# A fused two-block transformer kernel: the second pair of modulation slabs is loaded and multiplied ahead of the first projection's first products

## The chip, the cores and the metric

The kernel runs on one core of a Trainium2 chip. That core has five engines: TensorE (PE in the profile, its weight loads PEld) multiplies matrices, VectorE (DVE), ScalarE (ACT) and GpSimd (POOL) work elementwise, and SyncE (SP) issues most transfers. They meet through semaphores alone. The metric is the device time of one execution in microseconds (us); less is better.

## The reference

The reference is one transformer block with a mixture of experts, and behind it two more layers that mix tokens, all of them in float32 on 256 tokens of 1024 features. Only its start matters here. The condition `c`, one vector of 1024, is passed through silu and multiplied with a matrix of 1024 x 6144; the result, `mod`, is cut into six vectors of 1024, of which the first two are `shift1` and `scale1`:

```python
mod = jax.nn.silu(c) @ w_ada[l] + b_ada[l]
shift1, scale1, gate1, shift2, scale2, gate2 = jnp.split(mod[:, None, :], 6, axis=-1)
h = rms_norm(x, g_norm1[l]) * (1.0 + scale1) + shift1
proj = h @ w_in[l]
```

Behind that come the two attentions of the block, their output projections, the router, 64 experts of which each token takes 8, and the two further layers.

## The kernel before

**Weights.** All weights are kept in memory as slabs of 1 MB (128 partitions x 2048 numbers), in the order in which the kernel wants them. In the fast memory there is a ring of 11 slots of a slab each. Code of TensorE's program asks for a slab where it uses it (`take_slab`, line 585, and `new_slab`, line 476), and so the order of asking is the order of loading. The n-th slab takes the slot of slab n - 11. SP's program (`load`, line 1637) walks through the slabs in that order: it waits until the slab that had the slot has been given back (`given_back`, line 1630) and then issues the load (line 1659). It does not skip: while it waits for one slot, the loads behind it are not issued.

**Three kinds of slabs at the start.** A modulation slab (`ada1`, 0 to 7) holds 256 columns of the modulation's matrix: slabs 0 to 3 make `shift1`, 4 to 7 make `scale1`. `ada_slab` (line 590) multiplies one with the silu of `c`, 8 products on quarters of the array, and the slab's slot is given back when its products are done. A projection slab (`in`, 0 to 7 here) holds 256 columns of `w_in`, and is multiplied with the tiles of `h`, which the program calls `hT` and `h1`: 8 feature tiles k of 128 x 256 tokens. A projection slab is given back only when its last product, that of k = 7 for the second half of the tokens, is done. A side slab (`ada1`, 8 to 23; `leave_to_vector`, line 616) is not for TensorE: DVE weighs it with a row of `c` (`weigh_slab`, line 2276; two long instructions to a slab), and gives it back.

**From modulation to h.** Slabs j and j + 4 are a pair, and make the batch `("first", j)`: shift and scale of two of the eight feature tiles. When the pair has been multiplied, ACT copies the result out of its bank (`ada_quarters`, line 1798, the copy is line 1804), TensorE folds the four quarters together (`ada_fold`, line 642, products on line 647), DVE adds the bias, makes the gain and scales two tiles of `x` (`ada`, line 2202, and `scale`, line 2236), and ACT adds the shift (`shift`, line 1817, on line 1821). Then `h1` has two tiles more. ACT's program has these steps in the order copy, two shifts, copy, two shifts, and DVE's likewise.

**The order of TensorE's work at the start** is written out by hand (lines 853 to 876). `two_ks(s, i)` multiplies projection slab s with feature tiles 2i and 2i + 1 for both halves of the tokens: four products, which the profile counts as 8, as it does all products of float32. It waits for those tiles and, at its first use, for the slab. Each slab s has two banks that collect its sums (0 and 1 for slab 0, 2 and 3 for slab 1), which ACT empties when they are complete (lines 1848 and 1849), so that slabs 3 and 4 can use them again.

**What ACT issues.** With the fourth batch ACT issues transfers of its own on its queue (lines 1831 to 1841): constants, vectors, a row of `c` in a copy for each partition (`c_row`), the biases of the attention, and two more rows. The silu of `c_row` (line 1852) stands in ACT's program between the emptying of projection slab 0's banks and that of slab 1's, and DVE's weighing waits for it (line 2288).

The first loads are, before the change: modulation 0, modulation 4, projection 0, modulation 1, 5, projection 1, modulation 2, 6, 3, 7, projection 2, projection 3, side slabs 0 and 1, projection 4, side slabs 2 and 3, projection 5, and so on.

Of the kernel before, what the change touches and what calls it, by code (L numbers as in the profile page):

```python
# [148 lines left out]
def build(nc, x_d, ctx_d, consts_d, consts2_d, vecs_d, pos_d, rpb_d, spat_d, router_d, crow_d, crow2_d, slabs_d, exp_d, out_d):  # L149
    with ExitStack() as ctx:  # L150
# [5 lines left out]
        def S(name):  # L156
            if name not in sems:
                sems[name] = ctx.enter_context(nc.semaphore(name))
            return sems[name]
# [29 lines left out]
        def cc(name, a=0, b=None):  # L189
            src, at = (cs, C_AT) if name in C_AT else (cs2, C2_AT)  # L190
            lo, hi = at[name]
            if src is cs2 and lo >= DFT_W:
                src, lo, hi = cs_late, lo - DFT_W, hi - DFT_W
            return src[:, lo + a:(hi if b is None else lo + b)]
# [160 lines left out]
        def done(eng, name):  # L355
            b, n = place[name]
            eng.wait_ge(psum_done[b], n + 1)

        def bk(name):
            return bank[place[name][0]]  # L360
# [128 lines left out]
        def ends(n, end):  # L489

            slab_end[n] = end
            let_go.append(n)
            if given:
                given[0].append(n)
# [37 lines left out]
        def ada_batch(which, j):  # L532

            if which == "ada1" and j < 8:
                return ("first", j % 4), j // 4
            for n, (w, lo, count) in ADA_BATCHES.items():
                if w == which and lo <= j < lo + count:
                    return n, j - lo

        def batch_size(batch):  # L540
            return 2 if batch in FIRST_BATCHES else ADA_BATCHES[batch][2]
# [7 lines left out]
        OTHER = (12, 13, 20, 14, 15, 16, 17, 18, 19, 21, 22, 23)  # L549
        PASSES = [(i, t, side) for i, j in enumerate(OTHER) for t in range(2) for side in range(2 if j < 20 else 1)]  # L550
        PASSES_TO = [sum(n <= i for n, _, _ in PASSES) for i in range(len(OTHER))]
        other_slabs = []
        READ_EARLY, DUMPED_EARLY = 10, 20
# [8 lines left out]
        def _(pe):  # L562
            mmul = nc.tensor.matmul

            def open_group(name, b):

                if uses[b]:
                    pe.wait_ge(psum_done[b], uses[b])
                place[name] = (b, uses[b])
                uses[b] += 1  # L570
                return bank[b]

            def close_group(ins, name):
                ins.then_inc(psum_full[place[name][0]], 1)
# [10 lines left out]
            def take_slab(src):  # L585

                n = ask(src)
                return arrived(n), n

            def ada_slab(which, j):  # L590

                w, n = take_slab((which, j))
                w = w.rearrange("p (k c) -> p k c", k=8)
                batch, r = ada_batch(which, j)
                first, last = r == 0, r == batch_size(batch) - 1
                if first:
                    open_group((batch, "quarters"), 6)
                o = bk((batch, "quarters"))
                at = 15 - r if which == "ada1" else 22 - 2 * r  # L600
                for kk in range(2):
                    for g in range(4):
                        mm = mmul(o[32 * g:32 * g + 32, 0:256], (silc if which == "ada1" else silc2)[:, 4 * kk + g, at:at + 32],
                                  w[:, 4 * kk + g, :], start=first and kk == 0, stop=last and kk == 1)
                    if kk == 1:
                        if last:
                            close_group(mm, (batch, "quarters"))
                            ends(n, (batch, "quarters"))
                        else:
                            ada_reads[0] += 1  # L610
                            mm.then_inc(S("ada_read"), 1)
                            ends(n, ("ada_read", ada_reads[0]))
# [29 lines left out]
            def ada_fold(batch, b=7):  # L642

                done(pe, (batch, "quarters"))
                o = open_group((batch, "columns"), b)
                for t in range(2):
                    mm = mmul(o[:, 32 * t:32 * t + 32], quarters[:, t * P:(t + 1) * P], cc("fold"), start=True, stop=True)
                close_group(mm, (batch, "columns"))
# [180 lines left out]
            def first_inputs(slab, t, ks):  # L829

                name = (f"qk{slab}", t)
                if slab not in in_at:
                    in_at[slab] = take_slab(("in", slab))[1]
                o = open_group(name, 2 * slab + t) if ks[0] == 0 else bk(name)
                for k in ks:
                    h_tile("h1", k)
                    mm = mmul(o[:, 0:256], hT[:, k, t * P:(t + 1) * P], eight(in_at[slab])[:, k, :], start=(k == 0), stop=(k == KT - 1))  # L837
                if ks[-1] == KT - 1:
                    close_group(mm, name)
                    if t == 1:  # L840
                        ends(in_at[slab], name)
# [7 lines left out]
            def two_ks(slab, i):  # L849
                for t in range(2):  # L850
                    first_inputs(slab, t, (2 * i, 2 * i + 1))
# [2 lines left out]
            ada_slab("ada1", 4)  # L854
            pe.wait_ge(S("fold_in"), 16)
            ada_fold(("first", 0))
            two_ks(0, 0)
            ada_slab("ada1", 1)
            ada_slab("ada1", 5)
            ada_fold(("first", 1))  # L860
            two_ks(1, 0)
            two_ks(0, 1)
# [2314 lines left out]
```

## Time and profile before

| | us |
|---|---|
| runs: median (lowest to highest of 3) | 1056.69 (1054.32 to 1059.71) |
| profiled execution, its own time | 1058.16 |
| its span, first to last instruction | 1056.3 |
| TensorE busy in the span | 1012.3 |
| DVE / ACT / POOL busy | 454.9 / 282.6 / 160.5 |
| moved in transfers | 336.59 MB, mean 319 GB/s |

The profile is one execution as the hardware profiler saw it. Times in its rows count from the start of the span. A granted clock of 1.00 is TensorE's full clock, 2.4 GHz, and 0.50 its other level, 1.2 GHz. The share of transfers is the mean busy share of the core's 16 transfer engines; packets can overlap a little, so that a full stretch shows 1.01 or more. Queue q1 carries what SP issues, q10 what ACT issues. The idle time in brackets is that of the engine just before the instruction, with what ended it.

### The profile page before, as it was taken

The numbers are of one execution on the slowest core, as the hardware profiler recorded it, in microseconds if no ns is written. First come the engines' busy times: TensorE is split into PE (matmuls) and PEld (weight loads), VectorE is DVE, ScalarE is ACT, GpSimd is POOL, SyncE is SP. The second block draws the span as 40 slices with busy tenths as digits, with TensorE's granted clock in tenths as the row PEclk, the third lists the DMA queues.
The fourth block names the chain that finished last, engine by engine and source line by source line (L and its number), as shares of the span: only waits on it lengthen the run. The fifth ranks groups of instructions, "written<-read, shape, count | busy, mean of one in ns | idle before, by whom it ended". The sixth has DMA issues, their size and how long they took to land.

```text
span 1056.3 us, 16485 instructions
## 1 busy us (share of the span) xinstructions
PE 1012.3 (96%) x6434; PEld 712.6 (67%) x6434; DVE 454.9 (43%) x1112; ACT 282.6 (27%) x656; POOL 160.5 (15%) x154
## 2 busy tenths in 40 slices
PE   6998999999989999999899999999979999999998
PEld 4776867788546556465356556655459998998577
DVE  1366998686621321212112121221425652657941
ACT  3224465302511111212111211113222111213951
POOL 0000030225000000000000000001015963391001
PEclk9999999999999999999999999999989999999999
DMA  9999998469999999999999999999996434320001
GB/s 382 328 421 421 421 420 323 166 248 358 369 398 411 415 422 420 420 421 421 421 421 421 406 421 421 420 421 421 419 418 264 160 121 159 119 82 1 1 2 41
DMA packets 50463, 336.59 MB, mean 319 GB/s; under 512 B 5776, under 2 KB 8464, under 8 KB 10832
## 3 DMA queue, kind: packets, MB, share of 16 engines
q1 hardware_dynamic: 46976, 329.01, 76.8%
q10 hardware_dynamic: 3024, 4.79, 1.6%
q0 software_dynamic: 384, 1.70, 0.5%
q8 instruction: 53, 0.87, 0.3%
q14 instruction: 26, 0.21, 0.1%
HBM read 334.43 MB, written 1.05 MB: 318 GB/s over the span
## 4 chain that ended last, share of the span: by engine, by line
PE 85%; DMA 7%; DVE 4%; issue 2%; ACT 1%; SPq 0%; DVEq 0%; ACTq 0%
PE bank L1286 15%; PE bank L1447 11%; PE bank L1329 7%; PE bank L1241 5%; DMA ring<-experts 5%; PE bank L1107 4%; PE bank L1131 3%; PE bank L1174 3%; PE bank L1545 3%; PE bank L990 3%; PE bank L696 3%; PE bank L1598 2%; DMA ring<-stream 2%; PE bank L837 2%; PE bank L763 2%; PE bank L1007 2%
## 5 line engine op out<-in xcount | busy, mean ns | idle before, releaser
L1286 PE MATMUL bank<-ring,arena 128*32 128x512 f32 (+1 forms) x1112 | 175.8, 601 | 9.9 <-DMA ring<-experts 9.9
L1286 PEld LDWEIGHTS bank<-ring,arena 128*32 128x32 f32 (+1 forms) x1112 | 51.1, 120 | 114.7 <-issue 114.5
L1734 POOL TENSOR_TENSOR hT<-hT 128x256 f32<-128x256 f32 x30 | 28.5, 950 | 610.5 <-ACT hT L1815 608.8
L1329 PE MATMUL bank<-ring,conds 128*32 128x512 f32 (+1 forms) x560 | 87.8, 596 | 5.7 <-DMA ring<-experts 3.1
L2745 DVE TENSOR_TENSOR yhalf<-bank,yhalf 128x512 fp32r<-128x512 f32 x48 | 33.2, 692 | 80.0 <-ACT yhalf L2049 80.0
L2730 DVE SCALAR_TENSOR_TENSOR conds<-bank,gcol,conds 128x256 f32<-128x256 f32 x24 | 11.6, 484 | 123.8 <-ACT conds L2041 109.6
L2008 ACT ACTIVATE arena<-bank,mod 128x256 f32<-128x256 f32 x96 | 40.3, 471 | 78.2 <-PE bank L1107 77.9
L1329 PEld LDWEIGHTS bank<-ring,conds 128*32 128x32 f32 (+1 forms) x560 | 25.8, 119 | 49.9 <-issue 43.5
L1107 PE MATMUL bank<-picked,halves 128*128 128x256 f32 x384 | 57.8, 294 | 0.4 <-ACT arena L2008 0.4
L1107 PEld LDWEIGHTS bank<-picked,halves 128*128 128x128 f32 x384 | 49.0, 189 | 10.2 <-issue 9.1
L2488 DVE SCALAR_TENSOR_TENSOR resid<-bank,mod,resid 128x256 f32<-128x256 f32 x40 | 18.8, 482 | 80.3 <-PE bank L1174 25.4
L2041 ACT ACTIVATE conds<-bank 128x256 f32<-128x256 f32 x24 | 9.2, 383 | 144.5 <-PE bank L1286 144.5
L696 PE MATMUL bank<-hT,ring 128*128 128x256 f32 x192 | 42.5, 381 | 4.1 <-ACT arena L1901 2.2
L1131 PE MATMUL bank<-yhalf,selT 128*128 128x512 f32 x184 | 46.3, 394 | 0.0
L2283 DVE CUSTOM_DVE_ANT_1 hT<-ring,hT,ve 128x1024 bf16<-128x1024 f32 x32 | 40.3, 1307 | 10.5 <-DMA ring<-stream 10.5
L2049 ACT CAST yhalf<-bank 128x512 fp32r<-128x512 f32 x48 | 28.1, 585 | 60.5 <-PE bank L1329 60.5
L1241 PE MATMUL bank<-hT,ring 128*128 128x256 f32 x192 | 43.2, 382 | 0.0
L2737 DVE COPY conds<-bank 128x256 f32<-128x256 f32 x24 | 10.2, 425 | 76.3 <-PE bank L1316 76.3
L696 PEld LDWEIGHTS bank<-hT,ring 128*128 128x128 f32 x192 | 36.1, 190 | 10.1 <-DMA ring<-stream 5.4
L1815 ACT ACTIVATE hT<-resid 128x256 f32<-128x256 f32 x48 | 18.0, 411 | 88.6 <-DVE resid L2488 88.4
L1447 PE MATMUL bank<-hT,ring 128*128 128x128 f32 x304 | 40.5, 277 | 0.7 <-ACT hT L1821 0.7
L1241 PEld LDWEIGHTS bank<-hT,ring 128*128 128x128 f32 x192 | 36.0, 190 | 7.2 <-issue 2.5
(487 smaller groups left out, 1833.2 us busy)
## 6 DMA issues: line engine op xcount, KB each, us to landing
ring<-experts SPq DMA_DIRECT2D x187, 1024.0 KB, 13.1
ring<-stream SPq DMA_DIRECT2D x118, 1024.0 KB, 13.3
ring<-experts SPq DMA_DIRECT2D x8, 512.0 KB, 8.9
resid<-x SPq DMA_DIRECT2D x1, 1024.0 KB, 5.2
arena<-c_rows ACTq DMA_DIRECT2D x2, 512.0 KB, 12.2
resid<-ctx ACTq DMA_DIRECT2D x1, 1024.0 KB, 9.2
keys_room<-experts SPq DMA_DIRECT2D x1, 1024.0 KB, 13.0
arena<-stream SPq DMA_DIRECT2D x1, 1024.0 KB, 14.4
```

The source lines that it names most:

```text
L696: mm = mmul(o[:, 0:n_tok], w[:, k, t * P:(t + 1) * P], hT[:, k, 0:n_tok], start=(k == 0), stop=(k == KT - 1))
L990: mm = mmul(o[:, 0:256], w[:, 512 * k + P * t:512 * k + P * t + P], yT[:, y0 + k, :], start=(k == 0), stop=(k == 3))
L1107: mm = mmul(o[:, 256 * (d % 2):256 * (d % 2) + n], halves[:, q, t, P * d:P * d + P], picked[:, t, 0:n], start=(t == 0 and q == 0), stop=(t ...
L1131: mmul(bank[b][:, :], selT[:, b // 2, :], yhalf[:, q, 512 * (b % 2):512 * (b % 2) + 512], start=m == 0 and q == 0, stop=False)
L1174: mm = mmul(o[:, 0:T], eight(n)[:, k, P * (d % 2):P * (d % 2) + P], y_c[:, k, :], start=(j == 0), stop=(j == KT - 1))
L1241: mm = mmul(o[:, 0:T], w[:, k, P * (i % 2):P * (i % 2) + P], hT[:, k, T:2 * T], start=(k == 0), stop=(k == KT - 1))
L1286: mm = mmul(o[at:at + n_slots, :], xg_of(m, kk)[:, at:at + n_slots], w[g][:, k, :], start=(kk == 0), stop=(kk == KT - 1))
L1329: mm = mmul(o[at:at + n_slots, :], aT[:, f, at:at + n_slots], w[g][:, 2 * c + f, :], start=(f == 0), stop=(f == 1))
L1447: mm = mmul(o[:, at:at + P], lhs[:, k, :], rhs[:, k, :], start=k == 0, stop=k == 3)
L2008: last = a.activation(to[:, i, 0:n], bk(("xg", j, c))[:, 256 * i:256 * i + n], ACT.Identity, bias=mod1[:, 24 + 2 * c + i:25 + 2 * c + i])
L2283: v.tensor_tensor_reduce(out=products[:, 2 * t:2 * t + 2, :].rearrange("p a (b c) -> p a b c", b=2), in0=ring[:, slot_of[n], 1024 * t:1024 ...
L2745: last = v.tensor_tensor(yhalf[:, 1, 512 * c:512 * c + 512], bk(("y", m, c))[:, :], yhalf[:, 0, 512 * c:512 * c + 512].bitcast(F32), ALU.s ...
```

## The change

The first use of projection slab 0, its products with feature tiles 0 and 1, is moved behind modulation slabs 1 and 5 in TensorE's program. With it the order of loading changes: these two modulation slabs become the third and the fourth load, and projection slab 0 the fifth. All else is the same.

```diff
             ada_slab("ada1", 4)
             pe.wait_ge(S("fold_in"), 16)
             ada_fold(("first", 0))
-            two_ks(0, 0)
             ada_slab("ada1", 1)
             ada_slab("ada1", 5)
+            two_ks(0, 0)
             ada_fold(("first", 1))
             two_ks(1, 0)
             two_ks(0, 1)
```

## Rows read from the trace of the kernel before

**Rows 1.** The page: transfer shares in 40 slices of 26.4 us; the chain by engine
```profile
DMA  9999998469999999999999999999996434320001
...
PE 85%; DMA 7%; DVE 4%; issue 2%; ACT 1%; SPq 0%; DVEq 0%; ACTq 0%
```

**Rows 2.** TensorE in order of time: start, us, line, tiles, count [idle before, releaser]
```profile
13.23 1.93 PE L603 MATMUL bank<-ring,conds 128*32 128x256 f32 x32
...
18.03 2.57 PE L837 MATMUL bank<-ring,hT 128*128 128x256 f32 x8 [1.67 <-ACT hT L1821]
...
20.53 2.96 PE L603 MATMUL bank<-ring,conds 128*32 128x256 f32 x32
...
23.99 0.63 PE L647 MATMUL bank<-cs,quarters 128*128 128x32 f32 x4 [0.50 <-ACT quarters L1804]
...
24.46 5.43 PE L837 MATMUL bank<-ring,hT 128*128 128x256 f32 x24
```

**Rows 3.** Windows: stretch, us, busy us by engine, granted clock, transfer share, GB/s
```profile
15.20:18.00 2.80, 0.60 (x4) 0.53 (x5) 2.26 (x5) 1.00 (x3) 0.00 (x0) 1.00 1.01 421
...
18.00:20.50 2.50, 2.47 (x8) 1.66 (x8) 0.00 (x0) 0.28 (x1) 0.00 (x0) 0.75 1.01 419
...
20.50:23.50 3.00, 2.99 (x33) 1.24 (x32) 0.00 (x0) 0.00 (x0) 0.00 (x0) 0.64 1.03 429
```

**Rows 4.** The chain of waits, 50 to 125 us: start, us, what
```profile
57.41 22.83 DMA ring<-stream
...
80.29 3.72 PE bank L904 x16
...
106.21 14.05 PE bank L696 x64
```

**Rows 5.** Windows, as rows 3, of two longer stretches
```profile
37.00:45.00 8.00, 8.00 (x46) 6.84 (x39) 3.19 (x15) 2.67 (x8) 0.00 (x0) 1.00 0.76 221
...
57.00:177.00 120.00, 113.85 (x675) 89.10 (x674) 98.96 (x226) 54.70 (x138) 13.38 (x18) 1.00 1.01 421
```

**Rows 6.** TensorE in order of time, as rows 2, 60 to 90 us
```profile
64.61 7.17 PE L711 MATMUL bank<-ring,hT 128*128 128x256 f32 x32 [0.28 <-DMA ring<-stream]
...
72.83 7.17 PE L696 MATMUL bank<-hT,ring 128*128 128x256 f32 x32 [1.04 <-DMA ring<-stream]
```

**Rows 7.** SP and transfers at 3.6 us: issue; KB, us from issue to landing
```profile
3.42 0.47 SPq L1659 DMA_DIRECT2D ring<-stream  x1
...
ring<-stream SPq DMA_DIRECT2D x1, 1024.0 KB, 14.9
```

**Rows 8.** SP's waits, 13 to 46 us (total, times, longest); its issues, 40 to 60
```profile
SPq L1659 <- PE bank L837: 28.5, 1, 28.5
...
44.09 14.23 SPq L1659 DMA_DIRECT2D ring<-stream  x12
```

**Rows 9.** ACT's queue (q10), 45 to 49, then 50 to 52 us: packets, MB, share
```profile
q10 hardware_dynamic: 767, 0.88, 107.3%
...
q10 hardware_dynamic: 75, 0.29, 36.8%
```

**Rows 10.** ACT's issues; transfers issued 30 to 44 us: KB each, us to landing
```profile
37.45 0.33 ACTq L1831 DMA_DIRECT2D cs<-consts  x1
...
38.78 0.66 ACTq L1834 DMA_DIRECT2D hT<-c_row  x1
...
cs<-consts ACTq DMA_DIRECT2D x1, 585.0 KB, 3.5
...
hT<-c_row ACTq DMA_DIRECT2D x1, 512.0 KB, 6.1
```

**Rows 11.** ACT and DVE in order of time, as rows 2, 45 to 62 us
```profile
46.10 1.06 ACT L1852 ACTIVATE hT<-hT 128x1024 f32<-128x1024 f32 x1
...
54.33 1.28 DVE L2283 CUSTOM_DVE_ANT_1 hT<-ring,hT,ve 128x1024 bf16<-128x1024 f32 x1 [3.99 <-DMA ring<-stream]
...
59.62 1.28 DVE L2283 CUSTOM_DVE_ANT_1 hT<-ring,hT,ve 128x1024 bf16<-128x1024 f32 x1 [2.13 <-DMA ring<-stream]
```

## The prediction

> **What bounds the kernel now.** I read the page first: the chain that ended last is TensorE for 85% of the span, and the row of transfer shares is full except in slices 7 to 9, 158 to 238 us, and at the end [rows 1]. TensorE busy says little, because the change touches only the first 60 us; what counts is which wait ends last there. So the second view is TensorE's instructions in order of time [rows 2]. The reader is to see three things: after the first fold (it ends at 18.03 - 1.67 = 16.36) TensorE idles 1.67 us for the first two feature tiles of h1; then come the first products and the second pair of modulation slabs, and another 0.50 us goes to the copy ahead of the second fold; and the two pieces between those gaps are slow, 2.57 us for 8 products and 2.96 for the slab pair, where 24 products take 5.43 later (1.81 per 8) and the earlier slab pair took 1.93. The third view, the windows, says why: the granted clock is 0.75 and 0.64 of full there [rows 3], so it sat at the lower of its two levels, 1.2 GHz, for part of it, after a stretch in which TensorE was busy 0.60 of 2.80 us.
>
> The fourth view is the chain of waits from 50 to 110 us [rows 4]: TensorE until 57.0, and then one load, issued at 57.41, that lands at 80.24 and on which the last projection tiles start at 80.29. Transfers run at 421 GB/s with a share of 1.01 from 57 to 177 us [rows 5], and TensorE waits for slabs in that stretch (0.28 us at 64.61, 1.04 at 72.83 [rows 6]). So between 57 and 80 us the landing of slabs sets the time. TensorE's gain before 57 is worth only as much as the slabs come earlier. Behind 80 the path runs over the latent sums, the reciprocal on DVE, the latent squares on ACT and back to TensorE at 106.21, and from there TensorE is the chain, with transfers that have room soon after (slices 7 to 9). A shift at 80 is therefore carried to the end.
>
> **The change part by part.** No instruction, byte or transfer is added or removed: 8 products move behind two slabs' 32 instructions in TensorE's order, and, since slabs are asked for in that order, one load moves behind two others in SP's queue.
>
> *TensorE's order.* Now: fold, wait 1.67, products 2.57, slab pair 2.96, wait 0.50, fold. After: the pair starts at 16.4 and ends near 18.3 at full clock (1.93); the products need h1 (ready at 18.0) and their own slab; the second copy runs on ACT beside the products, and the second fold follows without its wait. Saved: 1.67 + 0.50 = 2.17 us. If the clock no longer falls, since the emptiest stretch is filled, 2.57 - 1.81 = 0.76 and 2.96 - 1.93 = 1.03 go as well: 3.96 us. ACT is no obstacle: its second copy stands behind the two shifts, of which the first let TensorE go at 18.03, and the pair ends only then.
>
> *The landings it needs.* The first projection slab becomes the fifth load instead of the third. The fifth load is issued at 3.42 and lands 14.9 us later, at 18.3 [rows 7], when the products are due; the two modulation slabs take places three and four and land earlier. I price this at nothing; with a landing 0.5 us later it costs 0.5. TensorE thus reaches the slab of the sixth projection tiles 2.2 to 4.0 us earlier; I take 3.5.
>
> *The ring.* This is what decides. The ring has 11 slots, and SP waits in order. The 12th and 13th loads take the slots of the first two modulation slabs, which are free once the first pair is through. The 14th takes the slot of the first projection slab, which is in use until its last products, and SP stands there 28.5 us, until 44.1 [rows 8]. Meanwhile the queue runs dry: from 37 to 45 us the transfers have a share of 0.76 and move 221 GB/s [rows 5], mostly small ones that ACT issues from 37.45 on [rows 10]. After the change slots three and four hold modulation slabs that are free near 17.3 and 18.3. So the 14th and 15th load are queued before 19 us, and only the 16th waits for the first projection slab, until about 44.1 - 3.5 = 40.6. Two slabs of 1.05 MB at 421 GB/s are 2 x 2.49 = 5.0 us of work, so the queue is full until 42. The empty part of the stretch, 8 x (1 - 0.76) = 1.9 us, or 2.0 against the 1.01 of a full one, is filled, and all that comes behind lands 2.0 us earlier. The rest is no gain: ACT's transfers have to be moved too, and while they were, from 45 to 49, ACT's queue alone had a share of 107% [rows 9].
>
> Bounds: the gain is at most 5.0 us, if ACT's small transfers cost the stream nothing, and it can't exceed TensorE's own 3.96 plus the 1.3 us that it waits now for slabs between 57 and 80; at least 0, if the empty share moves elsewhere. The value is the accounting of the row itself, 2.0.
>
> *What is late next.* TensorE reaches the sixth projection slab near 60.3 but this lands near 64.6 - 2.0 = 62.6, so some 2 us of its gain turn into a wait there. The clock may fall as it did at 16 to 23 us; that cost 1.8 us, of which the wait of 1.04 ahead of the seventh slab, now TensorE's only slack, takes up more than half, so at most 0.8 us is lost at the landing near 78.
>
> *ACT's transfers.* ACT issues the constants (at 37.45 now) and the row of c (38.78) some 3.5 us earlier, but now behind two more slabs. The row of c lands today 6.1 us after its issue, at 44.9 [rows 10]; its silu gates ACT's next evictions and DVE's weighing of side slabs. The trace shows how the two queues share: the loads that SP issued from 44.09 on moved nothing before 49, while ACT's earlier transfers were served [rows 8, 9]; that is service nearly in the order of issue. Then constants and row (1.12 MB) come behind the 15th load: at the stream's 0.42 MB/us they land at 42.3 + 2.7 = 45.0 at the earliest, and with all of today's 44.9 - 37.45 = 7.4 us at 49.7 at the latest; I take the middle, 47.4. From that landing DVE needs 2.3 us until the silu is done (46.10 + 1.06 today) and about 6.2 for two side slabs, at two instructions of 1.28 each, and four short reductions, before it can begin the third side slab, which will be there at 59.62 - 2.0 = 57.6 [rows 11]. The waits that DVE has today (3.99 us for the second side slab, 2.13 for the third) are that cover. A landing up to 57.6 - 8.5 = 49.1 leaves the full gain, one at 51.1 none. I cost it at nothing; at the late end it is 0.6.
>
> The Trainium skill (DMA: Bandwidth & Descriptors, "Queues, rings and completion order") says that each DMA engine serves its queues in turn, packet by packet. By that rule the row of c would not stand behind the two slabs and the last rival below falls away. The stretch from 45 to 49 us, 107% for one queue with eight loads waiting in the other, speaks against it here, the 37% that ACT's queue had beside the stream from 50 to 52 us for it [rows 9]; the forecast's 2.0 us are the same by both, as the engines have no empty time either way.
>
> **The sum.** The profiled execution took 1058.16 us (span 1056.3 and 1.9 around it); less 2.0 it is 1056.2. It lies 1.5 above the median of the three runs, so for the median 1056.69 - 2.0 = 1054.7.
>
> **The rivals.**
> - *The stream gains more than its empty time* (22%): up to 4.0 us, TensorE's own gain: 1052.7. For: shares above 1 mean that packets overlap, and 37 to 45 moved only 221 GB/s, so ACT's slow packets may fit in beside large ones. Against: beside the stream (50 to 52) ACT's 0.29 MB took 37% of the time, 0.39 MB/us, no less than the stream's own.
> - *Nothing reaches the end* (15%): 1056.7. TensorE's gain turns wholly into waits for slabs between 57 and 80 us. For: share 1.01 from 57 on. Against: the empty stretch ahead of it.
> - *The row of c comes too late* (8%): slower. Place: ACT's silu of it, ahead of the second projection slab's evictions and DVE's first side slab. Behind both slabs, and then beside the 16th load at the 0.29 MB in 2 us that ACT's queue got from 50 to 52 [rows 9], its 1.12 MB take 7.7 us in place of 2.7: 49.7 + 5.0 = 54.7, 3.6 past the 51.1 that leaves nothing, so 1056.69 + 3.6 = 1060.3. For: the 16th load is issued only 5 us after them. Against: what ACT issued first was served first. Each further microsecond costs one.
>
> **How the numbers follow.** The forecast has 55%, with its own range 1052.5 to 1057. What a measurement of this kernel can tell from no change is about 0.5%, 5.3 us; the three runs alone spread over 5.4. None of the cases reaches that by its mean. Faster by more than 5.3 us needs the first rival at its upper end and scatter: 12%. Slower by as much needs the last with a landing past 56, or scatter: 5%. Within: 83%. The range takes in the first rival's mean and 2 us of scatter below, and above the second with 2: 1050.5 to 1058.8, with the last and some scatter left out.
>
> **What would show it.** TensorE without the gaps of 1.67 and 0.50, granted clock near 1.0 from 16 to 23.5; SP's long wait for the first projection slab shorter than 28.5 and ended near 41; a transfer share near 1 from 37 to 45; the load that now lands at 80.24 landing near 78.2; a new wait of about 2 us ahead of the sixth projection slab; TensorE's restart at 106.21 near 104.2. Wrong would be: that landing unmoved (nothing gained), moved by 4 (the first rival), or DVE idle for ACT's silu past 50 us and the third side slab weighed after 59.6 (the last).

## The result, and the profile after

The changed kernel took 1071.74 us (median of 4 runs, 1066.90 to 1072.49) against 1058.20 for the kernel before beside it (4 runs, 1054.32 to 1061.78): ratio 1.0112, 95% interval 1.0073 to 1.0151. It is slower by more than 0.5%, where 1054.7 was forecast. The profiled execution took 1071.74 (span 1069.9), 13.6 more than the one of before; at 46 us it is still ahead, at 70 us 13.2 behind.

TensorE in order of time, changed kernel (start, us, line, operation, tiles, shapes, count, idle before and what ended it), the answer to [rows 2, 6]:

```profile
15.65 1.93 PE L603 MATMUL bank<-ring,conds 128*32 128x256 f32 x32
18.45 1.99 PE L837 MATMUL bank<-ring,hT 128*128 128x256 f32 x8 [0.87 <-DMA ring<-stream]
20.93 5.45 PE L837 MATMUL bank<-ring,hT 128*128 128x256 f32 x24
36.00 10.61 PE L837 MATMUL bank<-ring,hT 128*128 128x256 f32 x48
60.83 9.63 PE L885 MATMUL bank<-ring,hT 128*128 128x256 f32 x32 [14.22 <-ACT pr L1849]
70.30 7.07 PE L683 MATMUL bank<-ring,hT 128*128 128x256 f32 x32
77.20 7.07 PE L711 MATMUL bank<-ring,hT 128*128 128x256 f32 x32
```

The kernel before, from its last fold on:

```profile
39.50 10.61 PE L837 MATMUL bank<-ring,hT 128*128 128x256 f32 x48
49.94 7.07 PE L885 MATMUL bank<-ring,hT 128*128 128x256 f32 x32
57.15 7.17 PE L683 MATMUL bank<-ring,hT 128*128 128x256 f32 x32
```

The first four lines of the changed kernel are what was forecast, but for a wait of 0.87 us: the slab pair at full clock behind the fold, no gaps of 1.67 and 0.50, and the products behind the last fold begin at 36.0, 3.5 us earlier than they did. Then comes a hole of 14.22 us. L837 is projection slabs 0 to 2, L885 is slab 3, L683 slab 4, L711 slab 5. Slab 3 collects in the banks of slab 0, so it may start only when ACT has emptied these (L1848, L1849), and ACT has not. The windows show the two ends of it: the stretch in which transfers had a share of 0.76 [rows 5] is full now, and TensorE's clock sat at the lower level (0.50 of full is 1.2 GHz) from the hole until 65 us, so slab 3 took 9.63 us where the next took 7.07 (columns as in [rows 3]):

```profile
37.00:45.00 8.00, 8.00 (x39) 7.04 (x38) 0.47 (x2) 0.91 (x2) 0.00 (x0) 1.00 1.02 410
47.00:61.00 14.00, 0.17 (x1) 0.20 (x2) 2.40 (x13) 0.96 (x4) 0.00 (x0) 0.56 1.03 389
61.00:65.00 4.00, 4.00 (x10) 3.19 (x11) 1.36 (x3) 3.42 (x7) 0.00 (x0) 0.50 1.04 365
```

Why ACT was late is in its own row of instructions (ACTq marks the issuing of a transfer):

```profile
33.95 0.33 ACTq L1831 DMA_DIRECT2D cs<-consts  x1
...
35.28 0.64 ACTq L1834 DMA_DIRECT2D hT<-c_row  x1
...
38.19 5.82 ACTq L1839 DMA_DIRECT2D bias_room<-rpb  x1
44.04 15.95 ACTq L1841 DMA_DIRECT2D arena<-c_rows  x2
60.04 0.38 ACT L1848 ACTIVATE arena<-bank 128x256 f32<-128x256 f32 x1 [22.01 <-issue]
62.55 1.06 ACT L1852 ACTIVATE hT<-hT 128x1024 f32<-128x1024 f32 x1
```

ACT stood 22 us in issuing: the second bias transfer took 5.82 us to issue, the two later rows 15.95, where each of the same issues took 0.33 to 0.66 in the kernel before. The copies that TensorE waited for stand behind these in ACT's order. The chain of waits says the same (start, us, what):

```profile
38.19 5.82 ACTq L1839
...
44.72 15.27 ACTq L1841
...
60.83 9.63 PE bank L885 x32
```

And what ACT had issued before was late too. Transfers by issue (KB each, median us from issue to landing), against 3.5 and 6.1 in [rows 10]:

```profile
bias_room<-rpb ACTq DMA_DIRECT2D x2, 438.0 KB, 31.7
...
cs<-consts ACTq DMA_DIRECT2D x1, 585.0 KB, 9.5
hT<-c_row ACTq DMA_DIRECT2D x1, 512.0 KB, 24.7
```

The row of c, issued at 35.28, landed at 59.98, 15 us later than before. The two queues from 36 to 60 us (q1 is SP's, the stream; q10 is ACT's: packets, MB, share of the 16 engines):

```profile
q1 hardware_dynamic: 1131, 8.23, 85.4%
q10 hardware_dynamic: 1133, 1.36, 16.7%
```

Over the span: projection slab 3 is 10.9 us late (49.94 to 60.83) and slow, slab 4 13.2 late (57.15 to 70.30); the waits for slabs of [rows 6] are gone, so the restart of [rows 4] comes at 116.84, 10.6 late. The clock falls once more there (64 products take 15.74 us for 14.05), which makes it 12.3; a longer wait for the experts' loads at 322 us makes it 14.6, and at the end it is 13.6.

### The profile page after: what moved, and what is told of

The parts are those of the page before. It is cut to its first block, busy times and chain, and to the rows that moved or that the text cites. A ratio compares the mean times of both kernels' runs of the same rounds, so it can differ in the third digit from the quotient of the medians.

```text
span 1069.9 us, 16485 instructions
## 1 busy us (share of the span) xinstructions
PE 1014.3 (95%) x6434; PEld 714.2 (67%) x6434; DVE 455.9 (43%) x1112; ACT 282.8 (26%) x656; POOL 163.7 (15%) x154
## 4 chain that ended last, share of the span: by engine, by line
PE 83%; DMA 7%; DVE 4%; ACTq 2%; issue 2%; ACT 1%; SPq 1%; DVEq 0%
PE bank L1286 14%; PE bank L1447 11%; PE bank L1329 7%; PE bank L1241 5%; DMA ring<-experts 5%; PE bank L1107 4%; PE bank L696 3%; PE bank L1131 3%; PE bank L1174 3%; PE bank L1545 3%; PE bank L990 3%; PE bank L1598 2%; PE bank L763 2%; PE bank L1007 2%; PE bank L637 2%; PE bank L749 2%
## 5 line engine op out<-in xcount | busy, mean ns | idle before, releaser
L1734 POOL TENSOR_TENSOR hT<-hT 128x256 f32<-128x256 f32 x30 | 28.5, 950 | 612.9 <-ACT hT L1815 611.2
L1329 PEld LDWEIGHTS bank<-ring,conds 128*32 128x32 f32 (+1 forms) x560 | 26.0, 121 | 53.1 <-issue 47.2
## 6 DMA issues: line engine op xcount, KB each, us to landing
ring<-experts SPq DMA_DIRECT2D x187, 1024.0 KB, 13.4
```

The lines of the kernel that those rows point to most:

```text
L1329: mm = mmul(o[at:at + n_slots, :], aT[:, f, at:at + n_slots], w[g][:, 2 * c + f, :], start=(f == 0), stop=(f == 1))
```

## The experiments

Two theories to begin with. **A:** the transfer engines take a piece from each queue in turn; as long as SP's queue isn't dry, ACT's small pieces get one turn per 8 KB of stream, and the row of c, the issues behind it and the evictions behind those are late. **B:** the share goes by bytes or by order of issue, and the cause is elsewhere: in the products' new order, in the new order of loads as such, or in ACT's issuing. In the first four expectations A is called theory Q, there with ACT's held issues as what costs the time; rival P is the order of the products, and rival C is that the late landing of the row of c costs the time by itself. (Some expectations call L885 the second projection slab; it is slab 3.)

**Loads in the changed order, products in the old.** The two modulation slabs are asked for ahead of the first products, and used where they were:

```diff
+            asked = ask(("ada1", 1)), ask(("ada1", 5))
             two_ks(0, 0)
-            ada_slab("ada1", 1)
-            ada_slab("ada1", 5)
+            ada_slab("ada1", 1, asked[0])
+            ada_slab("ada1", 5, asked[1])
```

> The two modulation slabs are asked for ahead of the first projection slab, as in the changed kernel, but TensorE multiplies in the order of the kernel before. Theory Q (queue): with the stream's queue never dry, the bias transfers that ACT issues, small pieces, get only one piece for each 8 KB piece of the stream; ACT's next issue instructions then do not finish, ACT sits in them some 15 to 21 us, the first projection's banks are emptied late, and TensorE waits for them. So: 8 to 15 us slower than before, an issue on ACT of over 10 us, TensorE waiting some 10 us ahead of the fourth projection slab. Rival P (products): the order of TensorE's work is the cause; then this kernel is within 2 us of before and ACT's issues are short.

**Products in the changed order, loads in the old.**

```diff
             ada_fold(("first", 0))
+            early_in[0] = ask(("in", 0))
             ada_slab("ada1", 1)
             ada_slab("ada1", 5)
             two_ks(0, 0)
```

> TensorE multiplies in the order of the changed kernel, but the first projection slab is still asked for, and so loaded, third. Theory Q: SP waits for its slot as before, the stretch from 37 to 45 us stays free for ACT's transfers, ACT's issues take under 1 us each; the time is 0 to 2 us below before, since the slabs' landings between 57 and 80 us move little. Rival P: 10 to 14 us slower, as the changed kernel.

Measured, beside 1058.54 of before: loads alone 1065.42 (10 runs; eight of them 1065.2 to 1066.9, two at 1053.3 and 1055.8), ratio 1.0045 (1.0011 to 1.0079); products alone 1058.66, ratio 0.9994 (0.9969 to 1.0020). The loss comes with the order of loads, in eight of ten executions and not all of it. With the products alone TensorE's gain turns into waits for slabs, as the forecast's second rival had it (TensorE in order of time):

```profile
55.11 7.17 PE L683 MATMUL bank<-ring,hT 128*128 128x256 f32 x32 [1.11 <-DMA ring<-stream]
64.09 7.17 PE L711 MATMUL bank<-ring,hT 128*128 128x256 f32 x32 [1.81 <-DMA ring<-stream]
```

With the loads alone the row of c lands at 50.1, 5 us late, its silu runs 4 us late, and the two later rows, issued last, hold ACT a second time (ACT in order of time, in an execution of the longer kind):

```profile
50.13 1.06 ACT L1853 ACTIVATE hT<-hT 128x1024 f32<-128x1024 f32 x1 [1.72 <-DMA hT<-c_row]
...
73.89 1.06 ACT L1855 ACTIVATE arena<-arena 128x1024 f32<-128x1024 f32 x1 [12.30 <-DMA arena<-c_rows]
```

The issue of over 10 us and the wait ahead of slab 3 that were expected did not come: ACT's longest issues took 1.48 us, and 2.33 for two, and TensorE's wait, 8.74 us, lies inside slab 5, for copies that stand behind the silu of the later rows.

**ACT's held issues taken out of the way.** The changed kernel, with the bias and the two later rows issued behind the emptying of slab 1's banks and their silu moved back. If ACT's issuing is the root, the loss goes.

```diff
+                if s == 1:
+                    ...  # the four act.dma_start of bias and rows
...
-            act.wait_ge(S("bias_in"), 64)
-            ...  # silu of the two rows, now behind the vna copies
```

> The changed kernel, with ACT's four issues of bias and rows moved behind the eviction of the second projection slab, and the wait for them behind the evictions of the value tiles. Theory Q: nothing stands between the first fold's work and the evictions any more; TensorE has no wait of 14 us ahead of the fourth projection slab; 0 to 4 us below before, by the 2 us of transfer time that the full queue gains. Rival C (row of c): its landing, 60.0 us in the changed kernel, is what counts, through the silu ahead of the second projection slab's evictions; if it still lands past 55, TensorE waits at the fifth projection slab instead and the kernel stays 5 to 12 us slower.

1074.97 us, ratio 1.0149 (1.0116 to 1.0182): no better, as rival C had it. ACT in order of time:

```profile
59.53 1.06 ACT L1847 ACTIVATE hT<-hT 128x1024 f32<-128x1024 f32 x1 [16.75 <-DMA hT<-c_row]
...
61.50 0.64 ACTq L1851 DMA_DIRECT2D bias_room<-rpb  x1
62.17 0.66 ACTq L1851 DMA_DIRECT2D bias_room<-rpb  x1
62.86 2.86 ACTq L1853 DMA_DIRECT2D arena<-c_rows  x2
```

The row of c is as late as ever with nothing behind it in its queue, so the held issues don't make the row late; issued with the row gone, the same four take 4.2 us in place of 22. TensorE now gets through slab 3 and stops at slab 4, which needs slab 1's banks, emptied behind the row's silu: it starts 4.8 behind the kernel before, and loses 10.79 us more where the silu of the later rows, issued at 63, is awaited (TensorE in order of time):

```profile
61.92 9.26 PE L683 MATMUL bank<-ring,hT 128*128 128x256 f32 x32 [8.18 <-ACT pr L1844]
...
100.42 2.93 PE L656 MATMUL bank<-arena,ones 128*128 128x256 f32 x6 [10.79 <-ACT arena L1867]
```

**Bias and later rows from SP's queue**, issued ahead of its 16th load; ACT keeps constants, positions, vectors and the row of c.

```diff
+                if n == 15:
+                    ...  # the four transfers, by sp.dma_start
                 load(n)
```

> The changed kernel, with the same four transfers issued by SP in the stream's own queue, ahead of the 16th load. Theory Q: they are served in their turn without a share by pieces, ACT is never held, and the stream loses only their own time: 0 to 4 us below before, bias and rows landed by 58 us. Rival C: as in the run with ACT's later issues, 5 us or more slower if the row of c still lands past 55. If it is not the issuing queue but the sheer amount of transfers in this stretch: some 10 us slower as the changed kernel.

1060.33 us, ratio 1.0016 (0.9985 to 1.0046): most of the loss is gone. SP's queue carries small pieces itself while the row of c is on its way, and from 44 to 48 us equal turns are equal bytes:

```profile
q1 hardware_dynamic: 516, 0.50, 56.2%
q10 hardware_dynamic: 525, 0.47, 55.3%
```

The row lands at 53.1, still late.

The next two runs change the size of one side's pieces, and with it the number of its transfers, and nothing else. **The row of c in pieces of 512 B** (the changed kernel otherwise):

```diff
-                    act.dma_start(c_row, crow_d...).then_inc(S("vec_in"), 16)
+                    for h in (0, 128):
+                        act.dma_start(c_row[:, :, h:h + 128], crow_d...[:, :, h:h + 128]).then_inc(S("vec_in"), 16)
```

> The changed kernel with the row of c written in two transfers of 512 B pieces (1024 of them) in place of one of 1 KB pieces (512); the bytes, their place in ACT's queue and all of the order stay. Theory A (while the stream's queue holds loads, the engines take one piece of ACT's queue for each 8 KB piece of the stream, so a transfer's time goes by its count of pieces): 512 further pieces at the 49 per us of 52 to 60 us in the changed kernel, faster once the stream's queue is dry at about 64 us: 4 us at 49, the other 316 at about 150 per us, so the row lands at 66 to 67 us in place of 59.98, TensorE restarts 5 to 7 us later than at 60.83, and the kernel takes 1076 to 1080 us against 1071.74 of the changed one. Theory B (service by bytes, or by the order of issue, or the wait is in ACT's issuing): the row lands at about 60 us as before and the time stays at 1071 to 1073.

**The stream in pieces of 4 KB**, loads 11 to 22 (the changed kernel otherwise):

```diff
-                    sp.dma_start(room, w).then_inc(slab_in[slot], 16)
+                    for c in ((0, 1024), (1024, 2048)) if n in SPLIT else ((0, 2048),):
+                        sp.dma_start(room[:, c[0]:c[1]], w[:, c[0]:c[1]]).then_inc(slab_in[slot], 16)
```

> The changed kernel with loads 11 to 22 of the stream issued as two halves each, in pieces of 4 KB in place of 8 KB; bytes, order and ACT's transfers stay as they are. Theory A (one piece of ACT's queue for each piece of the stream): a pair of pieces takes 0.18 us of an engine in place of 0.32, so ACT's queue gets some 87 pieces per us in place of 49, the row of c lands at 48 to 52 us in place of 59.98, TensorE's second projection slab starts 8 to 10 us earlier than at 60.83, and the kernel takes 1062 to 1068 us against 1071.74; the 1280 pieces behind the row then last to about 65 us and may hold ACT again. Theory B (the share goes by bytes, or ACT's queue is served last whatever the pieces): the row stays at about 60 us, the time at 1071 to 1073.

With 512 B pieces the row landed at 68.2 (forecast 66 to 67); the kernel took 1073.19 us, below the 1076 to 1080 expected of it: slab 3 waits for ACT's issues, which were over at 62.7, and so starts 2.7 us later, where 5 to 7 were expected; what is late by the row comes only behind that. Queues from 52 to 60 us in that run:

```profile
q1 hardware_dynamic: 424, 3.08, 93.2%
q10 hardware_dynamic: 420, 0.21, 9.4%
```

With the stream in 4 KB pieces the row landed at 52.0 (forecast 48 to 52), slab 3 started at 51.04, and the kernel took 1066.58 us (5 runs; ratio 1.0072, 1.0045 to 1.0099), 5.2 less than the changed kernel, for no byte less. TensorE, and the queues from 52 to 60 us:

```profile
51.04 8.52 PE L886 MATMUL bank<-ring,hT 128*128 128x256 f32 x32 [4.33 <-ACT pr L1851]
```

```profile
q1 hardware_dynamic: 591, 2.14, 83.0%
q10 hardware_dynamic: 590, 0.50, 21.3%
```

Halving one side's piece moved the row by 8 us one way, halving the other's by 8 us the other way; the counts stay equal. The pieces alternate one by one, too: if those of the run with 512 B pieces, 52 to 60 us, are strung into 16 engines by their start and end times in the trace, 787 of 828 are followed by a piece of the other queue. By bytes or by order of issue neither would have moved it. Theory A is shown, but for what holds ACT's issues, which stays open (last section).

**What the order is worth with the row early.** All of ACT's transfers of 33.95 to 60 us go into SP's queue: constants, positions, vectors and the row ahead of load 13, bias and later rows ahead of load 15 (changed order), or all ahead of load 13 (order of before).

```diff
+                if n == 13:
+                    ...  # cs, rq, ve, c_row by sp.dma_start
+                if n == 15:
+                    ...  # bias and later rows by sp.dma_start
                 load(n)
```

> The changed kernel with all that ACT issues from 33.95 us on put into SP's queue: constants, positions, vectors and the row of c ahead of load 13, the bias and the two later rows ahead of load 15. Theory A (only the alternation of two queues of unequal pieces made the row late): the row lands with the stream, by about 45 to 50 us, no wait of 14 us is left before the second projection slab, and the 2.0 us of the prediction come through: 1054.5 to 1056.5 beside a kernel before of 1058.5 (ratio 0.996 to 0.998). Theory B (the changed order itself, with its clock or its landings, costs something that e4 still hid): at or above the kernel before, 1058 to 1062.

> The order of the kernel before, with all that ACT issued from 33.95 us on put into SP's queue ahead of load 13. Theory A: the dry stretch of the stream's queue beside ACT's (44 to 49 us) goes, and the row comes no later than its 44.9 us: 1 to 2 us faster, 1056.5 to 1057.5 beside 1058.5. If this alone gives as much as the changed order with the same edit, the changed order is worth nothing of itself. Theory B (moving these bytes ahead of loads 13 on only makes the slabs later): 1059 to 1061.

Beside 1059.19: changed order 1061.99, ratio 1.0016 (0.9993 to 1.0040), a miss for theory A's numbers; order of before 1057.79, ratio 0.9988 (0.9966 to 1.0009), 1.4 us less where 1 to 2 were expected, but not told from no change. The changed order's twelve executions are of two kinds, seven at 1061.9 to 1063.7 us and five at 1054.0 to 1057.5; the profiled one is of the longer kind. In it the row's silu ran at 42.9, and the evictions were not late. But 1.9 MB of bias and rows (2 x 438 and 2 x 512 KB) now stood ahead of projection slab 5 in the one queue:

```profile
64.01 10.10 PE L711 MATMUL bank<-ring,hT 128*128 128x256 f32 x32 [3.57 <-DMA ring<-stream]
```

It waited 3.57 us, and the clock fell behind the wait (0.66 of full from 60 to 70 us): 10.10 for 7.07. Here an early TensorE in front of landings that didn't come earlier bought a wait, and the wait cost the clock. So the last two runs take those bytes out of the stretch: **bias and later rows only ahead of load 33**, ACT's silu of them behind the square root of the latent heads, in the changed order and in the old one.

```diff
-                if n == 15:
+                if n == 33:
                     ...  # bias and later rows by sp.dma_start
```

> The changed order with constants, positions, vectors and the row of c in SP's queue ahead of load 13, the bias and the two later rows only ahead of load 33, and ACT's silu of those rows moved behind the square root of the latent heads (about 1.5 MB leave the stretch in which TensorE waits for slabs). Theory A (landings between 57 and 80 us set the pace, some 0.4 MB per us): 1.5 MB less ahead of them is up to 3.7 us; 1053 to 1055 beside 1058.5 (ratio 0.995 to 0.997). Theory B (TensorE's own work and its clock bind there once the row is early): no more than the changed order with all on SP, 1055 to 1056.5.

> The order of the kernel before with the edits of the run just ahead of it (constants, positions, vectors and the row of c in SP's queue ahead of load 13, the bias and the two later rows ahead of load 33, ACT's silu of those behind the square root of the latent heads): the two differ in the changed order alone. In the changed order that kernel took 1055.73 us, its TensorE began the products behind the first latent norm at 99.99 us. Theory A (with the row early and the landings out of the way, TensorE's early 2 to 3.7 us come through to that point): it begins at 102 to 104 us here, and the kernel takes 1056.5 to 1058. Theory B (the landings from 57 us on set that point whatever the order): 100 us here too, and 1055 to 1056. Theory C (a later bound, the experts' first transfers at 295 to 312 us, which gave back 4.3 of 5.5 us in that run, takes what there is): the point at 102 to 104 us and yet the same end within 0.5 us.

Changed order: 1055.73 beside 1059.19, ratio 0.9971 (0.9949 to 0.9993), the only version whose interval lies below the kernel before, though by less than the 0.5% that tells it from no change. Its time lies in theory B's range, 0.7 above theory A's; but the wait for projection slab 5 is gone, and the ratio is 0.0045 below that of the run with these bytes in the stretch, so they did cost time there. Order of before: 1058.40 beside 1059.48, ratio 0.9989 (0.9968 to 1.0010), with the restart where theory A had it and the time 0.4 above its range. TensorE restarts behind the latent squares (106.21 in [rows 4]) at 99.99 and at 102.41; here the changed order, then the order of before:

```profile
60.35 7.07 PE L711 MATMUL bank<-ring,hT 128*128 128x256 f32 x32
...
99.99 7.14 PE L696 MATMUL bank<-hT,ring 128*128 128x256 f32 x32 [3.77 <-ACT arena L1899]
...
304.87 3.64 PE L1329 MATMUL bank<-ring,conds 128*32 128x512 f32 x32 [2.06 <-DMA ring<-experts]
...
311.35 3.65 PE L1286 MATMUL bank<-ring,arena 128*64 128x512 f32 x16 [2.84 <-DMA ring<-experts]
```

```profile
102.41 15.92 PE L696 MATMUL bank<-hT,ring 128*128 128x256 f32 x64 [3.77 <-ACT arena L1899]
```

So in these two executions the order is worth 2.4 us at that point, once nothing waits for ACT's queue and the slabs come in time. At the end the two runs' ratios differ by 0.0018, some 1.9 us, with intervals that overlap: its worth there isn't settled. In this one profiled execution (1058.57, the highest of the twelve) the lead of 5.5 us that it had over the kernel before at 254 us was 3.9 at 275 and 1.2 at 312: part went in a stretch of low clock, the rest in waits for the experts' first loads, the last two lines of the changed order above. Whether that holds in the faster executions was not seen.

## Why the prediction was wrong

**TensorE's order: right.** 2.2 to 4.0 us were forecast, 3.5 taken; the products behind the last fold began 3.5 earlier, at a granted clock of 1.00 from 16 to 23.5 us. The size goes by the execution: over the traces these products begin at 35.9 to 36.2 with loads and products in the changed order, and at 38.1 to 39.8 with TensorE in the order of before, always some 26.3 to 26.6 us behind the first slab pair, which began anywhere from 11.9 to 13.2.

**The landings it needs: right.** Priced at nothing, for a landing at 18.3; the products began at 18.45. Their wait of 0.87 us is TensorE being early in that execution: its first slab pair began at 12.60 in place of 13.23, and in the three traces where it began at 13.4 or 13.5 there is no such wait.

**The ring: right as far as it shows.** SP's long wait for the first projection slab is 22.6 us in place of the 28.5 of [rows 8], and the share from 37 to 45 us is 1.02 in place of 0.76. Whether all behind it landed 2.0 us earlier can't be told from the changed kernel, whose TensorE waits for no slab between 30 and 125 us. But the empty stretch that was to be won was what had kept ACT's transfers quick: beside a dry stream they had the engines to themselves.

**ACT's transfers, costed at nothing: the step that failed.** It put the landing of the row of c at 45.0 to 49.7 and took 47.4, from "service nearly in the order of issue"; it was 59.98. That reading came from 45 to 49 us [rows 9], a stretch that began with the stream's queue dry. The right row stood beside it: from 50 to 52 us both queues had work, and ACT's moved 75 pieces in the 2 us. The prediction used that row too, but by its MB (0.29), which were pieces of 4 KB, of the later rows. Counted in pieces it is 37.5 per us, and then the row's own 512 pieces alone take 13.7 us beside the stream, in place of the 2.7 us by their bytes, or at most today's 7.4, that the step gave to constants and row together.

**ACT's issuing: not in the prediction at all.** It moved two transfers of ACT's queue in thought and left out the four issues behind them. These held ACT 22 us in its own order, so that slab 0's banks, ahead of the row's silu in ACT's order, were late as well as slab 1's. The run that moved them tells the shares at TensorE: a late row alone puts slab 4 back by 4.8 us, with the held issues it is 13.2.

**The last rival** (8%, 1060.3) had a place that is shown, ACT's silu ahead of slab 1's banks, the direction, and the sign: DVE waited 12.07 us for that silu, past 50 us. Its price of 3.6 us was the same count by bytes. Its "against", that what ACT issued first was served first, was the misread row.

The sentence on the Trainium skill (DMA: Bandwidth & Descriptors, "Queues, rings and completion order": each engine serves its queues in turn, packet by packet) drew the wrong conclusion from the rule. The runs agree with turns (1131 to 1133 pieces, 424 to 420, 591 to 590), and turns are just what makes the rival come true: a queue of small pieces beside one of large pieces is served evenly in pieces and badly in bytes.

## What to carry to other kernels

When a change keeps a queue full that used to run dry, look at what the other queue moved in that gap, and price it in pieces, not bytes: beside a full stream it gets about as many pieces as the stream does. A transfer of 512 KB in 1 KB pieces then costs as many turns as 4 MB of stream in 8 KB pieces. Look also at what stands behind the issuing of transfers on an engine that computes: once its queue is held, so are the copies that another engine waits for.

## What the runs showed that was not expected

- Equal turns are not the whole of it. Where the stream's queue had run dry, ACT's pieces went on alone for some time after the stream's loads were issued again: in the run with the loads alone, loads were issued at 46.14 and behind, and from 46 to 49 us the stream moved nothing while ACT's queue moved 622 pieces; the kernel before shows it too [rows 8, 9], with 987 pieces from 44 to 49 us. As an estimate from these counts, 39 to 62 pieces for each of 16 engines had been taken on before. No run here varied that.
- One order of loads gave two results, 1053 to 1056 and 1065 to 1067 us, in one set of ten runs with nothing between, and the run with all on SP's queue did likewise. Only the longer kind was profiled. That it hangs on whether ACT's pieces meet a dry queue is a guess.
- An issue on ACT took 0.33 to 0.66 us in the kernel before, and 5.82 and 15.27 at the longest in the changed one: the second transfer of the later rows was issued at 59.99 in the changed kernel, when the row of c had landed. With the row in 512 B pieces it was issued at 62.7, before the row had landed (68.2), so it isn't that landing as such that lets it go; what does is open.
- A hole of 3.57 us in TensorE's work cost another 3.0 us in clock, one of 14.22 cost 2.6.
